# A smaller scratch for software DMAs, and its room used for an early load of the fourth pair's gate weights

## The reference

```python
h2 = rmsnorm(x, norm2_w[l]) * (1.0 + scale2) + shift2
# hierarchical_moe: the best of 4 groups, in it the best 2 of 8 experts, for each token
for e in range(N_EXPERTS):                       # 32
    act = jax.nn.silu(hf @ w_gate[e]) * (hf @ w_up[e])      # 1024 -> 256
    y = y + combine[:, e:e + 1] * (act @ w_down[e])         # 256 -> 1024
x = x + gate2 * y
```

## Time and profile before

| | us |
|---|---|
| median of 3 runs | 1304.03 (1301.66 to 1306.97) |
| the profiled execution | 1299.1 |
| its span, first to last instruction | 1297.2 |
| PE busy | 1214.1 (94%) |
| DVE busy | 558.9 (43%) |
| ACT busy | 308.0 (24%) |
| POOL busy | 247.9 (19%) |
| DMA, mean over the span | 164 GB/s |

### The profile page before, as it was taken

How to read it: one execution, slowest core, us unless ns; L and a number is a source line. 1 busy time by engine, 2 the same in 40 slices (tenths; PEclk the granted TensorE clock), 3 DMA queues, 4 the chain that set the end, 5 groups by cost and what they waited for, 6 DMA issues and landing times.

```text
span 1297.2 us, 13452 instructions
## 1 busy us (share of the span) xinstructions
PE 1214.1 (94%) x5000; PEld 686.6 (53%) x5000; DVE 558.9 (43%) x1430; ACT 308.0 (24%) x725; POOL 247.9 (19%) x216
## 2 busy tenths in 40 slices
PE   6999999999989999999999999999999969988885
PEld 3555444455544444588884446766664544433342
DVE  2114384477648751208982367512223532322221
ACT  4223644433310000224022245300000321111110
POOL 6100022345510000071510030311300012211100
PEclk8999999999999999999999999999999979998898
DMA  9625104223276513313132102202248489999995
GB/s 330 118 69 134 65 25 106 87 92 131 67 241 209 183 42 135 112 67 130 65 108 87 43 23 65 71 0 65 66 154 365 170 315 390 407 400 415 409 406 202
DMA packets 91495, 213.06 MB, mean 164 GB/s; under 512 B 20201, under 2 KB 50297, under 8 KB 79095
## 3 DMA queue, kind: packets, MB, share of 16 engines
q1 hardware_dynamic: 77760, 190.51, 39.6%
q0 software_dynamic: 10464, 19.01, 5.9%
q10 hardware_dynamic: 3200, 2.61, 0.6%
HBM read 205.73 MB, written 14.75 MB: 170 GB/s over the span
## 4 chain that ended last, share of the span: by engine, by line
PE 76%; SPq 9%; DVE 7%; DMA 3%; ACT 3%; issue 2%; ACTq 0%; POOL 0%; POOLq 0%; DVEq 0%
PE PS L2285 7%; SPq L2779 7%; PE PS L996 6%; PE PS L639 6%; PE PS L1413 4%; PE PS L2348 4%; PE PS L1493 4%; PE PS L1676 4%; PE PS L1678 4%; PE PS L2456 3%; PE PS L2910 3%; PE PS L1422 2%; DMA AN<-in_w_down 2%; PE PS L1722 2%; PE PS L1734 2%; PE PS L711 2%
## 5 line engine op out<-in xcount | busy, mean ns | idle before, releaser
L996 PE MATMUL PS<-HT,W 128*128 128x512 f32 x256 | 123.5, 605 | 1.8 <-ACT AN L1160 1.8
L1258 POOL TENSOR_SCALAR AN<-AN,SM 128x128 f32<-128x128 f32 (+3 forms) x64 | 72.5, 1140 | 195.6 <-DVE SM L1350 195.6
L1281 DVE SCALAR_TENSOR_TENSOR AN<-AN,COLA 128x256 f32<-128x256 f32 x168 | 85.9, 512 | 5.4 <-DMA AN<-in_w_ada 0.5
L2910 PE MATMUL PS<-AN,HT 128*64 128x512 f32 x192 | 62.0, 640 | 12.6 <-DMA X<-in_w_up 7.8
L639 PE MATMUL PS<-W,HT 128*128 128x512 f32 (+1 forms) x192 | 71.8, 536 | 0.0
L2989 DVE TENSOR_TENSOR HT<-HT,PS 128x256 f32<-128x256 f32 x16 | 6.7, 421 | 137.2 <-ACT HT L2967 137.2
L996 PEld LDWEIGHTS PS<-HT,W 128*128 128x128 f32 x256 | 44.1, 192 | 38.6 <-issue 35.0
L1413 PE MATMUL PS<-HT,W 128*128 128x512 f32 x128 | 58.1, 599 | 0.0
L2456 PE MATMUL PS<-W,AN 128*128 128x512 f32 x128 | 57.6, 597 | 0.0
L1240 ACT ACTIVATE AN<-PS,SM 128x128 f32<-128x128 f32 (+3 forms) x64 | 33.7, 526 | 93.8 <-DVE SM L1329 93.5
L2348 PE MATMUL PS<-AN,W 128*128 128x512 f32 x128 | 55.7, 593 | 0.1
(11 more groups left out here) (513 smaller groups left out, 2268.0 us busy)
## 6 DMA issues: line engine op xcount, KB each, us to landing
W<-in_w_in SPq DMA_DIRECT2D x14, 2048.0 KB, 9.0
W<-in_w_down SPq DMA_DIRECT2D x20, 1024.0 KB, 27.1
AN<-in_w_gate SPq DMA_DIRECT2D x17, 1024.0 KB, 24.4
AN<-in_w_up SPq DMA_DIRECT2D x17, 1024.0 KB, 28.0
AN<-in_w_ada SPq DMA_DIRECT2D x16, 1024.0 KB, 5.2
AN<-in_w_down SPq DMA_DIRECT2D x12, 1024.0 KB, 26.1
W<-in_w_gate SPq DMA_DIRECT2D x10, 1024.0 KB, 24.8
W<-in_w_up SPq DMA_DIRECT2D x10, 1024.0 KB, 27.6
```

The source lines that it names most:

```text
L996: t = pe.matmul(u.ap, w[:, c, tile(m)], hT[:, c, :], start=c == 0, stop=c == 7)
L1258: pool.tensor_scalar(PU[u % 5][:, 0:n], PU[u % 5][:, 0:n], RSUM[:, u:u + 1], None, ALU.mult).then_inc(*sc_pool.up(u))
L1281: dve.scalar_tensor_tensor(out=a, in0=wt[:, c, :], scalar=ca["c2"][:, c:c + 1], in1=a, op0=ALU.mult, op1=ALU.add).then_inc(*ada_dve.up(p, c))
L2910: t = pe.matmul(u.ap[r, :].rearrange("p (n f) -> p n f", n=2), XGT[e % 2][:, c, r], w_gu(3 * e + half)[:, c], start=c == 0, stop=c == 7)
```

## The change

The constructor of the program gets `dynamic_dma_scratch_size=4096`; its default is 16384 bytes of each partition. That leaves 12,288 bytes of each partition free, and the new buffer `EX` of 3072 fp32 numbers takes them, 1.5 MB in all. Ahead of part 0 SP now loads into it the gate matrix of pair 3's first expert and half of the second expert's. The other half still goes into buffer 1 at `first_pe`; the gate half of buffer 0 isn't loaded for part 9 any more. Pair 3 multiplies in the form with gates first.

```diff
+    EX = sbuf("EX", 3072)
...
+    early_in, rest_in = sig("early_gates_in", "rest_of_early_gates_in", step=16)
...
         for n, w in enumerate((wg_, wu_)):
             for m in (3 * e, 3 * e + 1):
+                if e == EARLY and n == 0:
+                    if m % 3:
+                        ws.wait_ge(*first_pe.at())
+                        sp.dma_start(WE[m % NE][:, 1024:2048],
+                                     w[expert_of(e, 1)].rearrange("(p c) f -> p (c f)", c=8)[:, 1024:2048]).then_inc(*rest_in.up())
+                    continue
...
+    EARLY = NE // 3
+
+    def early_gate(half, c):
+
+        if half and c > 3:
+            return w_gu(3 * EARLY + 1)[:, c, 0]
+        return EX[:, 2048 * half + 256 * c:2048 * half + 256 * c + 256]
+
+    def sp_early(sp, ws):
+        for half in range(2):
+            sp.dma_start(EX[:, 2048 * half:(2048, 3072)[half]],
+                         wg_[expert_of(EARLY, half)].rearrange("(p c) f -> p (c f)", c=8)[:, 0:(2048, 1024)[half]]).then_inc(
+                             *early_in.up())
+
     def sp_experts(sp, ws):
+        sp_early(sp, ws)
...
-        if e in (0, NP - 2, NP - 1):
+        if e in (0, EARLY, NP - 2, NP - 1):
             for n in range(2):
-                if e:
+                if e == EARLY and n == 0:
+                    wp.wait_ge(*early_in.at())
+                    wp.wait_ge(*rest_in.at())
+                elif e == EARLY:
+                    wp.wait_ge(*exp_in[3 * e % NE].at(3 * e))
+                    wp.wait_ge(*exp_in[(3 * e + 1) % NE].at(3 * e + 1))
+                elif e:
...
-                        t = pe.matmul(u.ap[r, 256 * n:256 * n + 256], XGT[e % 2][:, c, r], w_gu(3 * e + half)[:, c, n],
-                                      start=c == 0, stop=c == 7)
+                        w = early_gate(half, c) if e == EARLY and n == 0 else w_gu(3 * e + half)[:, c, n]
+                        t = pe.matmul(u.ap[r, 256 * n:256 * n + 256], XGT[e % 2][:, c, r], w, start=c == 0, stop=c == 7)
...
-    nc = _bacc.Bacc("TRN2", target_bir_lowering=False, num_devices=1)
+    nc = _bacc.Bacc("TRN2", target_bir_lowering=False, num_devices=1, dynamic_dma_scratch_size=4096)
```

## The result

The changed kernel takes 1307.52 us (15 runs, 1304.70 to 1313.55), the one before 1303.55 us beside it (15 runs, 1296.93 to 1306.97). The ratio is 1.0046, with a 95% interval from 1.0032 to 1.0060: 4 to 8 us slower. (It isn't the quotient of the two medians, which lie 4.0 us apart; the means of the 15 runs, 1308.6 and 1302.6 us, lie 6.0 apart.) The forecast was 1302.1 us in a range that ended at 1306.5.

The account below looks back on a forecast made before the run. PE was taken to bound the kernel up to 1131.8 us, then SP's queue of expert weights. Terms 0 - 1.9 + 0 + 0 = -1.9 us took the median 1304.03 to 1302.1 us, range 1296.8 to 1306.5.

Parts of the forecast that it names:

- The smaller scratch: POOL's indirect DMAs in the experts' stage: the smaller scratch was taken to cost 0 us.
- The slower rival: Experts' scatter and gather loop: POOL waits for each indirect DMA to land; 79 us more, some 1383 us, chance 0.04.
- my 45: Experts' stage: at most five indirect DMAs under way at once, 45 packets for each DMA engine.
- The bytes taken out: SP's queue from first_pe (1058.42): 1.573 MB less, worth 3.98 us, of which 1.9 us was taken as gained.
- my caps: Backlog at the issues of 1061.88, 1068.73 and 1075.60, from landing times: gain limited to 3.8, 1.9 and 2.0 us.
- the second rival: Issues at 1068.73 or 1075.60: backlog is sharing with POOL's transfers, nothing gained; 1303.5 to 1304.5 us, chance 0.20.
- The early load: SP's queue ahead of the experts' first load: two DMAs, 4.1 us of transfer, fit an 8.0 us gap; cost 0.
- Pair 3 with gates first: PE at 1093.7: 64 matmuls of 256 columns for 32 of 512, 0 to 0.3 us more, reaching nothing; cost 0.
- From there to the end: From 1131.6 on SP's full queue sets the pace, so the 1.9 us gain comes through in full.
- near 400: Reading of the page before: the last eight GB/s slices stand near 400, most of the span at 20 to 240.
- 1297.5 to 1310.5: Sign for the whole kernel: a time outside these bounds in us would say that a mechanism is missing altogether.

Follow-up runs that it names:

- run 6: The changed kernel with the fourth small line load (124 KB) moved from POOL's queue to SP's; 1301.90 us, ratio 0.9994 against the kernel before.
- run 7: The kernel before with scratch at 4096 bytes and the fourth small line load on SP, without the early load; 1301.49 us, ratio 0.9995.
- run 5: The changed kernel, fourth small line load on SP, freed buffer room refilled at first_pe with three quarters of pair 4's gates; 1297.19 us, ratio 0.9952.
- run 1: The kernel before with the scratch at 4096 bytes and nothing else changed; 1308.43 us, ratio 1.0044.
- run 8: The kernel before with the scratch at 6144 bytes, nothing else changed; one run of 1300.09 us.
- run 2: The changed kernel with the 1 MB load of the bias lines issued by SP instead of POOL; 1299.72 us, ratio 0.9965 against the kernel before.
- run 3: The kernel before with the scratch at 8192 bytes and nothing else changed; 1302.72 us, ratio 0.9999.
- run 4: The kernel before, scratch as it was, with the 1 MB load of the bias lines issued by SP; 1302.13 us, ratio 0.9992.

## Why the prediction was wrong

*The smaller scratch, taken at 0.* This is the step that failed, and it alone explains that the time went up. I worked it out only where the change works, in the experts' stage. There it was right: the indirect issues stayed at 1.0 and 1.6 us. But the scratch is shared by all that POOL issues in the program, and its fullest moment is at 30 us. The slower rival had the right mechanism (POOL stands until earlier DMAs have landed) and the wrong place and price: 79 us in a loop, where it was one stall of 16 us that made PE 9.1 us late. The trace of before could have told: five POOL loads issued within 6.1 us and landing 14 to 17 us later, the last at 52.0, with PE's use at 57.43; 2321 packets on the software queue from 29 to 56 us, 145 an engine if they spread evenly, against my 45. The Trainium skill, DMA: Bandwidth & Descriptors (Terms), has a descriptor at 16 bytes, and my estimate from it was 256 an engine for 4096 bytes. The trace does not bear out the use I made of it: 145 packets are below 256, and POOL stood nevertheless. So packets are no measure of the fill, or they did not spread evenly, or more than these counted; no run tells which.

*The bytes taken out, gain 1.9.* Wrong in size: it was about 0 (runs 6 and 7, and the 1.65 MB of idle time). The method, a cap by the least backlog, was right; the backlogs were not. The summed deficit gives them: 0.6 MB by 1073, 1.2 by 1081, 1.65 by 1105. So of the 4.0 us taken out about 2.4 were left behind the ups, 1.0 behind the downs and none behind pair 4's gates, where my caps were 3.8, 1.9 and 2.0. I had taken each landing above 4.7 us as queue. The landings after, at the issues that answer to 1061.88, 1068.73 and 1075.60 in the earlier trace rows:

```profile
AN<-in_w_up SPq DMA_DIRECT2D x1, 1024.0 KB, 4.8
...
AN<-in_w_down SPq DMA_DIRECT2D x1, 1024.0 KB, 5.0
...
W<-in_w_gate SPq DMA_DIRECT2D x1, 1024.0 KB, 7.0
```

The first two find the queue empty. The third lands after 7.0 us, although only the two down loads had been issued since the engines were idle, and the second of them lands 0.8 us after this issue. Before, the second down load landed 3.3 us after the issue and the load of the third row took 6.7. So its landing time doesn't follow the queue. The likely rest is sharing with the scatter and the gather issued 5 and 3 us earlier; that is argued from the rows, no run tests it. The outcome is that of the second rival (nothing gained, chance 0.20). At 1061.88, where I forecast 3.8 us of queue against 4.0 taken out and so next to no gap, the share fell to 0.73: that backlog too was overstated, by more than a microsecond.

*The early load, cost 0.* Right. Two transfers are issued at 970.12, behind `w_out_2`. Issuing them takes 3.65 us where I had 0.4 to 0.5 each, but is done before the experts' first load is released at 976.69. The experts' stream ends at about 1014, and the DMA engines then rest until 1019.8, some 6 us, where they had rested for 8.0:

```profile
1015.00:1019.00 4.00, 4.00 (x23) 2.77 (x22) 0.76 (x4) 3.74 (x6) 0.00 (x0) 1.00 0.01 2
```

*Pair 3 with gates first, cost 0.* Right: in the chain its 64 matmuls take 6.91 us beside 6.87 for a pair of the other form, and none waits.

*From there to the end, in full.* Right as far as the runs go: the tail moved 406 GB/s from 1140.5 to 1289, as before, and where bytes were really saved (run 5) they came through, 3.3 of 3.9 us.

*What ends the stall.* The third small load is issued at 33.6 (the three take 3.92 us from 30.99) and is the last to land of the four loads issued before the stall. Its row, and that of the same load in run 1, issued at 33.7:

```profile
AN<-scr_line POOLq DMA_DIRECT2D x1, 124.0 KB, 17.1
```

```profile
AN<-scr_line POOLq DMA_DIRECT2D x1, 124.0 KB, 18.6
```

They land at 50.7 and 52.3, and POOL goes on at 51.05 and 52.69, 0.35 and 0.4 us later. So it looks as if POOL goes on only when everything that it had issued has landed, although the 1 MB load had landed at 44.5. A wait for the third small load alone would give the same times. Both profiles show this; no run was made to test it.

*The end of the program.* Not in the sum at all: 2.3 us of span that the smaller scratch gives back. Of the 9.1 us lost this leaves 6.8; measured were 6.0 (4.2 to 7.8). The 9.1 is itself good to some 2 us: in the eight profiles without the stall the 38.79 us run begins anywhere from 60.5 to 63.5.

*The readings and signs.* Of the last eight GB/s slices, which the prediction has "near 400", six are; the first is 315 and the last 202. And the measured 1307.52 us lies inside the 1297.5 to 1310.5 beyond which I would have said that a mechanism is missing. One was missing all the same: it was the chain of waits that showed it, and not the time.

What stays open: how many bytes of scratch the five loads fill was only bracketed, between 4096 and 6144 (runs 1 and 8); four small ones alone, or the 1 MB load with three, fit in 4096 (runs 2 and 6). What makes the end of the program shorter wasn't looked for. And the middle of the kernel, from the start of the 38.79 us run to pair 0's gates, is not the same in all profiles: 989.9 to 990.2 us in before, after and runs 1 and 3, but 992.5 to 993.8 in runs 2, 4, 5, 6, 7 and 8. The scratch doesn't sort them, as both groups have 4096 and 16384 bytes. The move of a line load to SP doesn't either, as run 8 has none. With one profile of each kernel it isn't known whether this is a matter of the kernel or of the execution. It is larger than most steps discussed here, so spans of single profiles were compared only stretch by stretch.

## What to carry to other kernels

A resource that is set once for the whole program has to be priced at its fullest moment, wherever that is, and not at the place of the change: list every DMA of the software queue with issue and landing, and look for where the most are under way. A wait of TensorE can cost more than its length, as here 2.3 us of matmuls at the lower clock came behind 7.3 us of idling. Bytes taken out of a saturated queue are worth something only if the queue stays non-empty through the next issues that are tied to an engine's pace; otherwise put other bytes in their place at once (run 5). What a landing takes beyond that of an empty queue is not the backlog, and here it overstated it each time: part of it can be another queue's traffic on the same engines.

## What the runs showed of the hardware that was not expected

The end of the program takes time that grew with the scratch of the software DMAs in these profiles: 1.7, 2.3, 3.3 and 3.9 us after the last landing at 4096, 6144, 8192 and 16384 bytes. And a scratch that was too small for the loads under way didn't make the program fail: POOL stood in front of the next issue, 16.1 and 17.7 us in the two profiles, and the profile puts it down to "issue", without a releaser.
